# FFN heads of a two-block transformer kernel: operands of two products made from a third's on VectorE, and value blocks transposed ahead of the scores

## What is computed

```
def swiglu(x, w_gate, w_up, w_down):
    return (jax.nn.silu(x @ w_gate) * (x @ w_up)) @ w_down

f1 = swiglu(rms_norm(x, ffn1_pre_g[l]), ffn1_w_gate[l], ffn1_w_up[l], ffn1_w_down[l])
x = x + FFN_RESIDUAL_WEIGHT * rms_norm(f1, ffn1_post_g[l])
```

```
z = jnp.einsum('bthd,bshd->bhts', q_blk, k_ctx) * (SB_HEAD_DIM ** -0.5)
log_keep = jnp.where(before, jax.nn.log_sigmoid(-z), 0.0)
csum = jnp.cumsum(log_keep, axis=-1)
weights = jnp.where(before, jnp.exp(jax.nn.log_sigmoid(z) + csum[..., -1:] - csum), 0.0)
return jnp.einsum('bhts,bshd->bthd', weights, v_ctx)
```

## Time and profile before

| | us |
|---|---|
| median of 3 runs (3801.39 to 3804.07) | 3803.8 |
| the profiled execution, its whole time | 3803.22 |
| its span, first to last instruction | 3801.4 |
| PE busy in the span | 3688.6 |
| DVE, POOL, ACT busy | 2344.4, 1690.4, 1655.0 |

### The profile page before, as it was taken

The page is one execution under the profiler, slowest core; times in us unless marked ns, Lnnn a source line. Parts: engine busy times, 40 slices in busy tenths (PEclk is TensorE's granted clock), DMA queues, the critical chain, the costliest instruction groups (busy, mean ns, idle before and its releaser), DMA issues.

```text
span 3801.4 us, 50433 instructions
## 1 busy us (share of the span) xinstructions
PE 3688.6 (97%) x19892; PEld 3041.5 (80%) x19892; DVE 2344.4 (62%) x3120; ACT 1655.0 (44%) x2839; POOL 1690.4 (44%) x1108
## 2 busy tenths in 40 slices
PE   8999999999999999999999899999999999999988
PEld 6888888666666566888888799999968998888877
DVE  7667784633455438667784866644487437666763
ACT  5333344433223335333443454411383346666663
POOL 4555554244444535555554144322351234444464
PEclk9999999999999999999999999999999999999989
DMA  3234574200000121234574011131121310000024
GB/s 123 97 108 153 170 263 154 90 19 27 23 19 21 51 82 63 97 108 153 180 256 151 25 43 50 40 117 51 48 72 58 123 51 25 29 31 31 25 71 145
DMA packets 143916, 327.29 MB, mean 86 GB/s; under 512 B 16896, under 2 KB 20512, under 8 KB 143296
## 3 DMA queue, kind: packets, MB, share of 16 engines
q1 hardware_dynamic: 132368, 281.80, 22.4%
q0 software_dynamic: 8752, 39.65, 2.8%
q10 hardware_dynamic: 2560, 2.61, 0.2%
HBM read 252.37 MB, written 71.63 MB: 85 GB/s over the span
## 4 chain that ended last, share of the span: by engine, by line
PE 81%; DVE 11%; ACT 5%; POOL 2%; issue 2%; ACTq 0%; DMA 0%; DVEq 0%; POOLq 0%
PE ps L958 7%; PE ps L960 7%; PE ps L959 7%; PE ps L414 5%; PE ps L415 5%; PE ps L416 5%; PE ps L977 4%; PE ps L978 4%; PE ps L976 4%; PE ps L4357 3%; PE ps L4282 3%; PE ps L2063 3%; PE ps L4284 2%; PE ps L4283 2%; PE ps L2065 2%; PE ps L2064 2%
## 5 line engine op out<-in xcount | busy, mean ns | idle before, releaser
L388 POOL TENSOR_TENSOR wlo<-raw,whi 128x1024 fp32r<-128x1024 f32 x154 | 377.5, 2455 | 485.3 <-ACT whi L379 485.0
L414 PE MATMUL ps<-xh,whi 128*128 128x352 f32 (+1 forms) x1400 | 472.9, 338 | 6.3 <-DVE xl L671 2.7
L415 PE MATMUL ps<-xh,wlo 128*128 128x352 f32 (+1 forms) x1400 | 450.7, 322 | 0.0
L416 PE MATMUL ps<-xl,whi 128*128 128x352 f32 (+1 forms) x1400 | 449.7, 321 | 0.0
L861 POOL TENSOR_TENSOR fwl<-fpb,fwh 128x512 fp32r<-128x512 f32 x204 | 301.2, 1486 | 267.8 <-ACT fwh L851 267.4
L861 POOL TENSOR_TENSOR fwl<-fpa,fwh 128x512 fp32r<-128x512 f32 x202 | 294.7, 1467 | 277.3 <-ACT fwh L851 277.2
L4664 POOL TENSOR_TENSOR ospl<-osp,osph 128x672 fp32r<-128x672 f32 (+4 forms) x144 | 189.9, 1320 | 328.2 <-ACT osph L4485 325.7
L414 PEld LDWEIGHTS ps<-xh,whi 128*128 128x128 f32 x1400 | 264.8, 189 | 17.4 <-POOL wlo L388 5.4
L415 PEld LDWEIGHTS ps<-xh,wlo 128*128 128x128 f32 x1400 | 264.4, 189 | 7.8 <-issue 1.9
L416 PEld LDWEIGHTS ps<-xl,whi 128*128 128x128 f32 x1400 | 264.3, 189 | 0.0
L958 PE MATMUL ps<-fxh,fwh 128*128 128x512 f32 x640 | 249.1, 389 | 0.7 <-ACT u L1036 0.7
(11 more groups left out here) (509 smaller groups left out, 9675.0 us busy)
## 6 DMA issues: line engine op xcount, KB each, us to landing
raw<-in_w_dram SPq DMA_DIRECT2D x154, 512.0 KB, 3.7
hs_scratch<-u SPq DMA_DIRECT2D x176, 256.0 KB, 2.4
u<-hs_scratch SPq DMA_DIRECT2D x118, 256.0 KB, 2.8
fpa<-in_fg_dram SPq DMA_DIRECT2D x88, 256.0 KB, 3.8
fpb<-in_fg_dram SPq DMA_DIRECT2D x88, 256.0 KB, 4.0
fpa<-in_fd_dram SPq DMA_DIRECT2D x88, 256.0 KB, 3.2
fpb<-in_fd_dram SPq DMA_DIRECT2D x88, 256.0 KB, 3.8
acc<-hs_scratch SPq DMA_DIRECT2D x80, 256.0 KB, 2.8
```

What stands on the lines that cost most here:

```text
L388: pool.x.tensor_tensor(K.wlo[n % 3][:, :], K.raw[n % 2][:, :], K.whi[n % 3][:, :], ALU.subtract).then_inc(*S.up("w_lo", n))
L414: pe.x.matmul(out, wh, xh, start=k == 0, stop=False)
L415: pe.x.matmul(out, wl, xh, start=False, stop=False)
L416: last = pe.x.matmul(out, wh, xl, start=False, stop=k == K - 1)
```

## The change

Four things are changed.

1. The activation sums of M7 and M4 are made from M6's, each by one VectorE operation for a row block: M7's is x(k,1) g(k) plus M6's sum, with the sign turned; M4's is x(k+4,1) g(k+4) plus M6's sum. ScalarE's 8 scalings and GpSimd's 8 subtractions of each FFN are gone. M6's low part, which overwrites M6's sum, now comes after both.
2. In the head the steps are put in another order: the weight steps 4 and 5 go ahead of the activation sums on ScalarE (in both FFNs) and on GpSimd (in the second); M4's sum goes to right behind std(1,0); on ScalarE the copies of M1 and M5 go ahead of the Silu of std(1,1).
3. The weight sum of step 17 (M6 of tile 3) moves behind VectorE's read of M7's bank.
4. In `ODD_PLACES` "turn" goes ahead of "z" and "mask".

The transposes now have the scores between them and the projection. The core of the diff:

```diff
@@ act_ffn
     pre = norms[0].pre
-    for n in (4, 5):
-        act_operand(act, f, n)
     std(0, 0)
     for n in (6, 7):
         act_operand(act, f, n)
     act_mix(act, f, "M6", "hi", pre)
-    act_mix(act, f, "M7", "scale", pre)
     std(0, 1)
...
     for n in (10, 11):
         act_operand(act, f, n)
+    act_mix(act, f, "M4", "hi", pre)
+    beside(STD, "M1")
+    beside(STD, "M5")
     std(1, 1)
     late_done(act, norms)
-    for n in range(FIRST_GATE, NSTEP):
-        if n > FIRST_GATE + 2:
-            act_operand(act, f, n + 4)
+    for n in (12, 13):
+        act_operand(act, f, n)
+    act_operand(act, f, 14)
+    beside(STD, "M6")
+    for n in range(FIRST_GATE + 3, NSTEP):
+        act_operand(act, f, n + 4)
@@ dve_mix, part "sum"
-            elif m == "M7":
-                ins = dve.x.scalar_tensor_tensor(t, K.res[:, 4 + i, META:META + 512], g4, t, ALU.mult, ALU.subtract)
             else:
-                dve.wait_ge("pool_mixsum", (f, "M4", i, 1))
-                ins = dve.x.scalar_tensor_tensor(t, K.fyh[:, i, 0:512], g4, t, ALU.mult, ALU.add)
+                dve.wait_ge("dve_mixsum", (f, "M6", i))
+                if m == "M4":
+                    dve.wait_ge("pe_group", ("u", f, 1, 0))
+                k, w = (i, g) if m == "M7" else (4 + i, g4)
+                ins = dve.x.scalar_tensor_tensor(t, K.res[:, k, META + 512:META + 1024], w, mixed(K, "M6", i)[2],
+                                                 ALU.mult, ALU.add)
@@ dve_ffn
     std(0, 0)
     std(0, 1)
-    dve_mix(dve, f, "M6", "lo", pre)
     dve_mix(dve, f, "M7", "sum", pre)
     raw_sum(dve, f, 9)
     std(1, 0)
     late_done(dve, norms)
+    dve_mix(dve, f, "M4", "sum", pre)
+    dve_mix(dve, f, "M6", "lo", pre)
     raw_sum(dve, f, 10)
     raw_sum(dve, f, 11)
     dve_mix(dve, f, "M7", "lo", pre)
+    raw_sum(dve, f, 12)
     std(1, 1)
-    raw_sum(dve, f, 12)
+    dve_mix(dve, f, "M4", "lo", pre)
...
-        if n + 5 < FIRST_DOWN:
+        if n == FIRST_GATE + 5:
+            raw_sum(dve, f, n + 4)
+        if n + 5 < FIRST_DOWN and n != FIRST_GATE + 4:
             raw_sum(dve, f, n + 5)
-        if n == FIRST_GATE + 1:
-            dve_mix(dve, f, "M4", "sum", pre)
-        if n == FIRST_GATE + 3:
-            dve_mix(dve, f, "M4", "lo", pre)
@@ pool_ffn
+    for n in range(4) if f == 1 else (4, 5):
+        pool_operand(pool, f, n)
     for L in norms:
         for k in range(8):
             rows_ready(pool, L, k)
-    pool_mix(pool, f, "M5")
-    for n in range(4, 10):
+    pool_mix(pool, f)
+    if f == 1:
+        for n in (4, 5):
+            pool_operand(pool, f, n)
+    for n in range(6, 12):
         pool_operand(pool, f, n)
-    pool_mix(pool, f, "M4", 0, 2)
-    pool_operand(pool, f, 10)
-    pool_mix(pool, f, "M4", 2, 3)
-    pool_operand(pool, f, 11)
-    pool_mix(pool, f, "M4", 3, 4)
@@ act_in (first FFN)
+    for n in (4, 5):
+        act_operand(act, 1, n)
     act_mix(act, 1, "M6", "scale", a.pre)
@@ act_out_end (second FFN)
     act_root(act, a, 1)
     act_root(act, b, 0)
+    for n in (4, 5):
+        act_operand(act, 2, n)
     for k in range(8):
         act_high(act, b, k)
@@ _odd_places
         out.extend(("out", it) for it in old[:split])
+        for it in new:
+            if it[1] < 7 and it[0] % PER_T in (12, 14, 16):
+                out.append(("turn", (it[1] + 1, it[0] % PER_T // 2 - 6)))
         out.extend(("z", it) for it in new)
         out.extend(("mask", it) for it in new)
         out.extend(("mix", it) for it in old[1:] if split)
-        for it in new:
-            if it[1] < 7 and it[0] % PER_T in (12, 14, 16):
-                out.append(("turn", (it[1] + 1, it[0] % PER_T // 2 - 6)))
```

More of the change, by code:

```diff
@@ L1008, in act_mix @@
         if part == "scale":
-            if m == "M4":
-                act.wait_ge("pool_mixsum", (f, "M4", i, 0))
-                scaled(t, t, i, (f, m, i, "scale"))
-            elif m == "M6":
-                scaled(t, K.res[:, 4 + i, META:META + 512], 4 + i, (f, m, i, "scale"))
-            else:
-                scaled(t, K.res[:, i, META:META + 512], i, (f, m, i, "scale"))
+            scaled(t, K.res[:, 4 + i, META:META + 512], 4 + i, (f, m, i, "scale"))
         elif m == "M5":
@@ L1020, in act_mix @@
             act.wait_ge("dve_mixsum", (f, m, i))
-            act.x.activation(hi, t, ACT.Copy, scale=-1.0 if m == "M6" else 1.0).then_inc(*S.up("act_mix", (f, m, i)))
+            act.x.activation(hi, t, ACT.Copy, scale=1.0 if m == "M4" else -1.0).then_inc(*S.up("act_mix", (f, m, i)))
 def act_ffn(act, f, norms, after):
@@ L1073, in act_ffn @@
         act_operand(act, f, n)
+    act_mix(act, f, "M4", "hi", pre)
+    beside(STD, "M1")
+    beside(STD, "M5")
     std(1, 1)
     late_done(act, norms)
-    for n in range(FIRST_GATE, NSTEP):
-        if n > FIRST_GATE + 2:
-            act_operand(act, f, n + 4)
+    for n in (12, 13):
[4 more added lines that the diff above has]
+        act_operand(act, f, n + 4)
         before = STEPS[n - 1]
-        if before[0] == "gate":
+        if before[0] == "gate" and n > FIRST_GATE + 3:
             beside(before[1], before[2])
-        if n == FIRST_GATE + 1:
-            act_mix(act, f, "M4", "scale", pre)
-        if n == FIRST_GATE + 2:
-            for late in (4, 5):
-                act_operand(act, f, FIRST_GATE + late)
-            act_mix(act, f, "M4", "hi", pre)
-            act_operand(act, f, FIRST_GATE + 6)
         act_row(act, f, n + 3)
@@ L1116, in dve_mix @@
         if part == "sum":
-            dve.wait_ge("act_mix", (f, m, i, "scale"))
             if m == "M6":
+                dve.wait_ge("act_mix", (f, m, i, "scale"))
                 dve.wait_ge("pool_mixsum", (f, "M5", i))
                 ins = dve.x.scalar_tensor_tensor(t, mixed(K, "M5", i)[2], g, t, ALU.mult, ALU.subtract)
-            elif m == "M7":
-                ins = dve.x.scalar_tensor_tensor(t, K.res[:, 4 + i, META:META + 512], g4, t, ALU.mult, ALU.subtract)
-            else:
-                dve.wait_ge("pool_mixsum", (f, "M4", i, 1))
-                ins = dve.x.scalar_tensor_tensor(t, K.fyh[:, i, 0:512], g4, t, ALU.mult, ALU.add)
+            else:
+                dve.wait_ge("dve_mixsum", (f, "M6", i))
[4 more added lines that the diff above has]
+                                                 ALU.mult, ALU.add)
             ins.then_inc(*S.up("dve_mixsum", (f, m, i)))
@@ L1131, in dve_mix @@
             ins = dve.x.scalar_tensor_tensor(lo, t, g, hi, ALU.mult, ALU.subtract)
-        elif m == "M6":
+        elif m == "M4":
+            ins = dve.x.tensor_tensor(lo, t, hi, ALU.subtract)
+        else:
+            if m == "M6":
+                dve.wait_ge("dve_mixsum", (f, "M7", i))
+                dve.wait_ge("dve_mixsum", (f, "M4", i))
             ins = dve.x.scalar_tensor_tensor(lo, t, -1.0, hi, ALU.mult, ALU.subtract)
-        else:
-            ins = dve.x.tensor_tensor(lo, t, hi, ALU.subtract)
         ins.then_inc(*S.up("dve_mixlo", (f, m, i)))
@@ L1273, in acc_ready, with pool_mix @@
     return "dve_acc", (f, (("M3", "M2"), ("M7", "M4"))[k // 4][c], k % 4)
-def pool_mix(pool, f, m, first=0, end=4):
+def pool_mix(pool, f):
     S, K = pool.S, pool.K
-    def rows(k, c):
-        return K.res[:, k, META + 512 * c:META + 512 * c + 512]
-    if m == "M4":
-        pool.wait_ge("pe_group", ("u", f, 1, 0))
-    for i in range(first, end):
-        t = mixed(K, m, i)[2]
-        pool.x.tensor_tensor(t, rows(i, 0), rows(i, 1),
-                             ALU.subtract).then_inc(*S.up("pool_mixsum", (f, m, i) if m == "M5" else (f, m, i, 0)))
-        if m == "M4":
-            pool.x.tensor_tensor(K.fyh[:, i, 0:512], rows(4 + i, 1), rows(4 + i, 0),
-                                 ALU.subtract).then_inc(*S.up("pool_mixsum", (f, m, i, 1)))
+    for i in range(4):
+        pool.x.tensor_tensor(mixed(K, "M5", i)[2], K.res[:, i, META:META + 512], K.res[:, i, META + 512:META + 1024],
+                             ALU.subtract).then_inc(*S.up("pool_mixsum", (f, "M5", i)))
 def pool_ffn(pool, f, norms, after):
-    if f == 1:
-        for n in range(4):
-            pool_operand(pool, 1, n)
+    for n in range(4) if f == 1 else (4, 5):
+        pool_operand(pool, f, n)
     for L in norms:
```

1 line of the change is left out of this document (removed).

## The result

The changed kernel takes 3779.95 us (median of 4 runs, 3775.84 to 3784.64), before took 3803.41 in the same measurement (4 runs, 3801.39 to 3804.07). The ratio is 0.9943, 95% interval 0.9931 to 0.9955, so 17 to 26 us less. The forecast was 3780. The profiled execution took 3777.27 for a span of 3775.5.

What follows compares the result with a forecast made beforehand. PE bounds the kernel, losing 10.7 and 12.4 us to waits in the FFN heads. Gains of 9.3 and 9.8 there plus 4.9 from the transposes, together 24.0, take 3803.8 to 3779.8, say 3780; range 3773 to 3791.

Steps and rivals of the forecast that it cites:

- (a): FFN heads: PE waits 1.31 and 2.90 us for weight step 4, which ScalarE writes behind activation sums and norm's root.
- Step 1: Both FFNs: GpSimd loses 8 operations of 1.7 us, ScalarE 8; std(1,1) and M4's sum no longer slowed.
- Step 2: FFN heads: weight steps 4 and 5 early remove PE's wait; price 1.9 us in the second head's norm chain, bounds 0 to 3.5.
- Step 3: FFN heads: copies ahead of the Silu end waits at M6 and M7; M4 then stands 1.4 us, second head 0.7.
- (b): First FFN head: PE waits 1.39 us ahead of M6 for the copy of M1, behind the Silu of std(1,1).
- (c): FFN heads: PE waits 4.82 and 4.59 us ahead of M7 for M6's copy, behind M4's operand on ScalarE.
- Step 4: Attention head pairs: transposes ahead of the scores remove PE's waits for the value copy; gain 4.9 us, bounds 3 and 5.6.
- VectorE as the bound in both heads: Rival, 18%: M4 stalls 4 us and the clock falls after it, 6 us per head; time 3789.7.
- handed back downstream: Rival, 6%: a late load or store takes the gain; only the transposes and half a head stay, 3793.
- slower: Rival, 4%: VectorE's 15 operations behind std(1,0) all collide with GpSimd, 5.7 us lost per head; time 3810.
- the edit that does nothing: Rival, 7%: M7 still waits, ScalarE being held ahead of M6's copy for step 12's weight sum; 3 us per head, 3786.
- nothing is late: Rival, 17%: no new wait in heads or transposes, gains 10.7, 12.4 and 5.6, together 28.7; time 3775.

Runs made afterwards that it cites:

- low_twice: Changed kernel with GpSimd making each low part of steps 8 to 11 twice; first head 77.7 us, 5.8 more than the changed kernel's.
- silu_first: Changed kernel with the copies of M1 and M5 put back behind the Silu of std(1,1); costs 0.3 and 0.2 us in the two heads.
- second measurement: Changed kernel, unchanged, run again beside the kernel before: 3783.26 us (5 runs), 17.9 us under before, ratio 0.9956.

## Why the prediction was right

The total was right: 3780 forecast, 3779.95 measured, and 22.5 us by stages against a sum of 24.0. Point by point:

- **What bounds the kernel; the waits counted.** Right. 10.7 and 12.4 us lost are what the stages show: head and rest together went down by 8.7 and 8.6, and what is left adds up below. Only the slow clock behind (a), one of the causes named, was none: it comes in some executions and moves the head by 0.2 us.
- **GpSimd's operations as VectorE's price.** Right, and shown: 1.05 us each in `low_twice`. By the rule of a full block (the Trainium skill, SBUF — State Buffer, Who interferes with whom), with 1.3 us for a GpSimd operation, these would by my estimate be 5.2 instead of 4.20 and, in the norm's chain, 2.6 instead of 2.1: the traces agree that the two engines hold each other up, and put the price lower.
- **Step 1, fewer operations.** The three plus four collisions that the walk counted ahead of the read are the ones in the rows of after (3.76 and 4.69 us for M4's sums and M7's low parts, 1.68 and 5.77 for the difference and M4's low parts). What the step is worth by itself is not shown, as no run undoes it alone.
- **Step 2, steps 4 and 5 early.** The price was right: 2.1 us against 1.9. What it is worth is less than its wait and the slow clock of the earlier trace rows suggest: undone, it costs only 1.1 us in the second head, where the clock stayed up. In the first head it was not undone.
- **Step 3, the gap ahead of M4.** The walk of VectorE's list was close: the read was to end at 86.4 with M1 at 68.8, it ended at 86.94 with M1 at 69.28. The gap costs 1.6 us with its restart in the first head (1.4 forecast) and 1.3 in the second (0.7 forecast); the second was mis-sized. No granted clock fell behind either.
- **Not in the sum.** The wait at M6 of tile 3, 0.4 us in each head with its restart (the rest of gate and up takes 359.4 and 359.5 us with it and 359.0 without). I stopped my walk at M4; the next thing late was one tile on. With it: 10.7 - 1.6 - 0.4 = 8.7, and 12.4 - 2.1 - 1.3 - 0.4 = 8.6.
- **What each edit is worth.** Here my words were wrong though the sum was not. I wrote that the copies ahead of the Silu let (b) and (c) go. `silu_first` shows that they do take (b) away, but that this is worth only 0.3 us: without them PE stands 2.0 us at M6 and no longer at M4. And they have no part in (c): M7 does not wait in `silu_first` either. What is left to take (c) away is M4's operand, which ScalarE now writes ahead of the copies (from 70.38 us on in after, from 82.95 in before) and without its scalings; that is read from the rows below, and no run takes this part out alone, though the wait of 4.82 us and the 1.6 us of slow clock behind it are 6.4 of the first head's 10.7. The weight sum of step 17, which I priced at 0.7 to 1.7 a head, is worth 3, as I left out that the sum has to wait for GpSimd, and that the clock falls after the longer gap.

ScalarE's high parts of M4 in the first head of before, which stand ahead of the copy of M6 (88.10) and wait there for VectorE's sums:

```profile
82.95 1.14 ACT L1021 ACTIVATE fxh<-fyl 128x512 fp32r<-128x512 f32 x2
84.85 0.63 ACT L1021 ACTIVATE fxh<-fyl 128x512 fp32r<-128x512 f32 x1 [0.77 <-DVE fyl L1125]
86.53 0.63 ACT L1021 ACTIVATE fxh<-fyl 128x512 fp32r<-128x512 f32 x1 [1.04 <-DVE fyl L1125]
```

And in after, with the copy of M6 at 77.75:

```profile
70.38 2.18 ACT L1015 ACTIVATE fxh<-fyl 128x512 fp32r<-128x512 f32 x4
...
77.75 0.57 ACT L1030 ACTIVATE u<-ps 128x512 f32<-128x512 f32 x1
```

- **Step 4, the transposes.** Right: 5.2 us against 4.9, bounds 3 to 5.6. PE's wait for `ovt` is down from 15 times to one, and no turn waits.
- **The rivals.** VectorE as the bound in both heads, handed back downstream, slower, and the edit that does nothing: none came, nor did "nothing is late".
- **The median within 1 us** was luck in part: the sum was 1.5 us too much, and in the second measurement the same pair was 17.9 apart.

The cause of the 8.5 us of scatter outside these stages stays open; only the mean clock was seen to go with the time of whole executions.
